# One ring of 1 MB weight pieces, adaLN split into steps by contraction tile and placed in the mixers, in a four-layer hybrid trunk on one core

## The reference, cut to what matters

```python
def trunk(x, cond, grid_rows, gla_s0, prm):
    for i in range(DEPTH):                       # 4 layers
        mod = (jax.nn.silu(cond) @ prm['w_ada'][i] + prm['b_ada'][i])[:, None, :]
        sh1, sc1, g1, sh2, sc2, g2 = jnp.split(mod, 6, axis=-1)
        h = rmsnorm(x, prm['norm_g'][i, 0]) * (1.0 + sc1) + sh1
        y = mixer_i(h)        # 0 Hyena convolution, 1 gated linear attention, 2 FNet, 3 pooling
        x = x + g1 * y
        h = rmsnorm(x, prm['norm_g'][i, 1]) * (1.0 + sc2) + sh2
        x = x + g2 * hier_moe(h, ...)            # 16 experts, two per token
    return rmsnorm(x, prm['final_g']), states
```

## Time and profile before

| what | value |
|---|---|
| median of 3 runs | 1601.7 us (1598.37 to 1603.82) |
| profiled execution | 1601.74 us, its span 1599.9 us |
| PE busy | 1414.2 us, 88% of the span |
| DVE, ACT, POOL busy | 394.0, 288.8, 100.7 us |
| DMA traffic | 552.35 MB of 10^6 bytes, mean 345 GB/s; 421 to 422 GB/s in the slices in which it never pauses |
| mean granted PE clock | 0.952 |

### The profile page before, as it was taken

How to read it: one execution, slowest core, us unless ns; L and a number is a source line. 1 busy time by engine, 2 the same in 40 slices (tenths; PEclk the granted TensorE clock), 3 DMA queues, 4 the chain that set the end, 5 groups by cost and what they waited for, 6 DMA issues and landing times.

```text
span 1599.9 us, 17267 instructions
## 1 busy us (share of the span) xinstructions
PE 1414.2 (88%) x7154; PEld 738.4 (46%) x7154; DVE 394.0 (25%) x904; ACT 288.8 (18%) x520; POOL 100.7 (6%) x105
## 2 busy tenths in 40 slices
PE   7999777799998799988799998888999865999986
PEld 3677335544432364857434433464444323444423
DVE  4333333412111320322411112123121124211112
ACT  2211000311010221112311101332110125111101
POOL 1000231110000100001100000011000012000001
PEclk9999978899999899999899999898999997899998
DMA  9877849489999976569499999685999996699995
GB/s 325 342 315 322 352 165 392 190 304 408 422 421 421 425 293 241 213 267 394 183 384 422 421 421 424 288 349 223 384 421 421 421 420 274 245 414 422 421 421 220
DMA packets 68671, 552.35 MB, mean 345 GB/s; under 512 B 7955, under 2 KB 8630, under 8 KB 10726
## 3 DMA queue, kind: packets, MB, share of 16 engines
q1 hardware_dynamic: 66266, 545.79, 83.0%
q0 software_dynamic: 1568, 4.55, 1.0%
q10 hardware_dynamic: 748, 0.74, 0.1%
HBM read 548.96 MB, written 2.10 MB: 344 GB/s over the span
## 4 chain that ended last, share of the span: by engine, by line
PE 71%; DMA 18%; DVE 6%; ACT 2%; issue 1%; POOL 1%; SPq 1%; DVEq 0%; POOLq 0%
PE bank L722 21%; DMA ring<-in_moe_w 15%; PE bank L671 12%; PE bank L746 10%; PE bank L631 6%; PE bank L690 4%; PE bank L706 3%; DMA ring<-in_w_ada 3%; PE bank L502 2%; PE bank L516 2%; PE bank L841 1%; PE bank L647 1%; PE bank L1008 1%; POOL hT L1827 1%; PE bank L904 1%
## 5 line engine op out<-in xcount | busy, mean ns | idle before, releaser
L722 PE MATMUL bank<-ring,arena 128*64 128x512 f32 x1024 | 236.9, 599 | 33.5 <-DMA ring<-in_moe_w 32.9
L722 PE MATMUL bank<-ring,hT 128*64 128x512 f32 x1024 | 226.3, 594 | 2.7 <-DMA ring<-in_moe_w 2.7
L746 PE MATMUL bank<-ring,arena 128*64 128x512 f32 x896 | 200.3, 596 | 0.2 <-DMA ring<-in_moe_w 0.2
L722 PEld LDWEIGHTS bank<-ring,arena 128*64 128x64 f32 x1024 | 68.6, 136 | 194.1 <-issue 125.2
L1419 DVE TENSOR_TENSOR rows<-rows,bank 128x512 f32<-128x512 f32 x32 | 22.0, 687 | 480.5 <-PE bank L722 480.5
L722 PEld LDWEIGHTS bank<-ring,hT 128*64 128x64 f32 x1024 | 71.7, 137 | 143.6 <-issue 134.5
L746 PEld LDWEIGHTS bank<-ring,arena 128*64 128x64 f32 x896 | 60.9, 137 | 119.6 <-issue 108.0
L671 PE MATMUL bank<-hT,ring 128*128 128x256 f32 x512 | 113.7, 383 | 1.7 <-DVE hT L1387 1.7
L631 PE MATMUL bank<-ring,condT 128*32 128x512 f32 x768 | 93.3, 641 | 16.8 <-DMA ring<-in_w_ada 16.8
L671 PEld LDWEIGHTS bank<-hT,ring 128*128 128x128 f32 x512 | 97.8, 192 | 15.8 <-issue 2.4
L1827 POOL TENSOR_TENSOR hT<-hT 128x256 f32<-128x256 f32 x48 | 34.7, 723 | 1029.2 <-ACT hT L1093 1026.0
(11 more groups left out here) (250 smaller groups left out, 1340.0 us busy)
## 6 DMA issues: line engine op xcount, KB each, us to landing
ring<-in_moe_w SPq DMA_DIRECT2D x368, 1024.0 KB, 18.1
ring<-in_w_ada SPq DMA_DIRECT2D x48, 2048.0 KB, 17.1
arena<-in_moe_w SPq DMA_DIRECT2D x16, 1024.0 KB, 23.4
ring<-in_hy_w_in SPq DMA_DIRECT2D x6, 2048.0 KB, 11.7
ring<-in_hy_w_out SPq DMA_DIRECT2D x2, 2048.0 KB, 19.1
ring<-in_gla_w_v SPq DMA_DIRECT2D x2, 2048.0 KB, 8.1
ring<-in_gla_w_g SPq DMA_DIRECT2D x2, 2048.0 KB, 8.1
ring<-in_gla_w_o SPq DMA_DIRECT2D x2, 2048.0 KB, 25.7
```

The source lines that it names most:

```text
L722: last = mm(bank[4 + kind][SLOTS * e:SLOTS * e + SLOTS, :], x[:, k, at:at + SLOTS], w[:, kk, e, :], start=k == 0, stop=k == KD - 1)
L746: last = mm(bank[6 + q // 2][SLOTS * e:SLOTS * e + SLOTS, :], hidT[:, f, SLOTS * e:SLOTS * e + SLOTS], w[:, ff, e, :], start=f == 0, stop= ...
```

## The change

The ring becomes 12 slots of 1 MB, used in strict turn by every piece. The mixers' weights are laid out in pieces of 256 columns in place of 512. An adaLN piece becomes one contraction tile k of all 2048 columns, so that eight pieces make a product, each used by itself in one step (4 matmuls) and freed by itself. The product (`ada(n, lo, hi)`) and the transposes (`ada_turned(n)`) stand apart on PE, as do `ada_rows` and `ada_mod` on DVE. Places: n = 0 before w_in; 1 to 4 in the Hyena convolution; 5 to 7 in GLA; 8 and 9 in FNet; 10 and 11 in pooling. n = 2 and 4 use bank 6, the others bank 7. The first gather of an expert stage uses banks 4, 6, 5, 6 in place of 4, 6, 7, 5, and its fourth part waits for the evacuation of its second. The arguments `beside` and, in `moe_round`, `turned` stand in the code and are not used.

The core of the diff:

```diff
-RING = 6
-PIECE = 4096
-SLAB = PIECE // 2
+RING = 12
+SLAB = 2048
...
+    before = [ada(0) + pieces("w_in", 12) + ada(1) + ada(2) + ada(3) + ada(4) + pieces("w_out", 4),
+              ada(5, 0, 5) + pieces("wq", 2) + ada(5, 5) + pieces("wk", 2) + pieces("wv", 4) + pieces("wg", 4)
+              + ada(6) + ada(7) + pieces("wo", 4),
+              ada(8) + ada(9) + pieces("fn", 4),
+              ada(10, 0, 5) + pieces("pool", 1) + ada(10, 5) + ada(11)]
...
+        experts = [("moe", i, p, kind, q) for p in range(PAIRS) for kind in range(3) for q in range(SLABS)
+                   if p or kind < 2]
+        for what in before[i] + [("first", i)] + experts + [("further", i)]:
...
-                return "ada_mm", 3 * what[1] + what[2] + 1
+                return "ada_mm", KD * what[1] + what[2] + 1
...
-                slots = [arrived(("ada", i, q, j)) for j in range(4)]
-                for k in range(KD):
+            def ada(n, lo, hi):
+                if lo == 0 and n:
+                    pe.wait_ge(s("mod_ready"), {2: 1, 3: 2, 4: 3}.get(n, n))
+                for k in range(lo, hi):
+                    w = arrived(("ada", n, k), 4)
                     for j in range(4):
-                        last = mm(bank[7][32 * j:32 * j + 32, :], condT[:, k, :], piece(slots[j], KD, 512)[:, k, :],
+                        last = mm(ada_bank(n)[32 * j:32 * j + 32, :], condT[:, k, :], w[:, j, :],
                                   start=k == 0, stop=k == KD - 1)
-                last.then_inc(s("ada_mm"), 1)
+                    last.then_inc(s("ada_mm"), 1)
+            def ada_turned(n):
                 pe.wait_ge(s("ada_rows"), n + 1)
...
             to_rows(0)
-            ada_at("w_in5")
+            ada(1, 0, 1)
             forward(0)
             to_rows(1)
-            ada_at("conv0")
+            ada(1, 1, 5)
             forward(1)
             inverse(0)
+            ada(1, 5, 8)
+            ada(2, 0, 3)
             to_rows(2)
+            ada_turned(1)
+            ada(2, 3, 4)
             forward(2)
             inverse(1)
+            ada(2, 4, 8)
+            ada(3, 0, 2)
             to_rows(3)
-            ada_at("conv1")
+            ada_turned(2)
+            ada(3, 2, 3)
             forward(3)
             inverse(2)
-            ada_at("conv2")
+            ada(3, 3, 8)
             inverse(3)
+            ada_turned(3)
+            ada(4, 0, 8)
             pe.wait_ge(s("z_ready"), 4)
-            residual(0, "w_out", rhs=uT)
+            residual(0, "w_out", rhs=uT, turned=4)
...
-        def first_gather(pre):
-            for t, b in enumerate((4, 6, 7, 5)):
+        def first_gather(pre, first):
+            for t, b in enumerate((4, 6, 5, 6)):
+                if t == 3:
+                    pe.wait_ge(s(pre + "xg_ready"), first + 2)
                 gather(pre, t, b)
...
+            ada(10, 0, 3)
             norm(6)
+            ada(10, 3, 5)
...
+            ada(11, 0, 8)
+            ada_turned(11)
             norm(7)
             moe(3)
```

More of the change, by code:

```diff
@@ L111, in constants @@
     return {k: v.astype(np.float32) for k, v in out.items()}
[L115 to L145, removed]
-            at += 1
[L148 to L158, removed]
-    return out
@@ L166, in build @@
+def build(nc, a):
+    stream = piece_stream()
+    where = {what: (slot, nth) for what, slot, nth in stream}
     ctx = ExitStack()
@@ L348, in source @@
                     "wk": "gla_w_k", "wv": "gla_w_v", "wg": "gla_w_g"}[k]
-            return a[name][what[1]]
+            return a[name][c]
         USED = ["h1_mm", "h3_mm", "y_mm"]
-        def landed(unit, part):
-            return s(f"{'fullb' if part else 'full'}{unit}")
         def expert_slab(n):
@@ L419, in _ @@
             last = {}
[L421 to L434, removed]
+            for what, slot, nth in stream:
                 if what[0] == "first":
@@ L469, in _ @@
                     continue
-                unit_free(unit, part)
-                src = source(what)
-                sp.dma_start(ring[unit][:, 0:src.shape[1]], src).then_inc(s(f"full{unit}"), 16)
-                last[unit, 0] = last[unit, 1] = freed(what)
+                if slot in last:
+                    name, value = last[slot]
+                    sp.wait_ge(s(name), value)
+                if what[0] == "moe":
+                    _, i, p, kind, q = what
+                    src = expert_slab(3 * SLABS * (PAIRS * i + p) + SLABS * kind + q)
+                else:
+                    src = source(what)
+                sp.dma_start(ring[slot][:], src).then_inc(s(f"full{slot}"), 16)
+                last[slot] = freed(what)
             for g, name in enumerate(("y_prompt", "y_sample")):
@@ L1325, in _ @@
[L1325 to L1334 removed]
+            norm(2)
+            shift(2)
@@ new lines, in _ @@
+            chain(last)
+            for b in range(2):
+                o_root = ors[:, 2 * b:2 * b + 2].rearrange("p h t -> p (h t)")
+                act_fn(o_root, o_root, ACT.Exp, scale=-0.5).then_inc(s("ors_ready"), 1)
+            residual(1, None, quarter)
+            moe(1)
+            norm(4)
+            shift(4)
+            for n in range(8):
+                act.wait_ge(s("mix_mm"), n + 1)
+                act_fn(fnp[:, n // 4, n % 4], bank[n % 4][:], ACT.Copy).then_inc(s("mix_rows"), 1)
@@ L1336, in _ @@
+            residual(3, "pool_b", half)
+            moe(3)
+            norm(2 * LAYERS)
             for g, name in enumerate(("y_prompt", "y_sample")):
```

800 lines of the change are left out of this document (403 added, 397 removed).

## The result

The changed kernel takes 1537.8 us in the median of 4 runs (1537.26 to 1539.11), against 1601.7 us (1598.37 to 1603.82): a ratio of 0.9604, with a 95% interval of 0.9586 to 0.9622. The forecast was 1538 us. The profiled execution took 1537.64 us, its span is 1535.8 us, 64.1 less than before.

The account below looks back on a forecast made before the run. No resource bounds throughout: PE and helpers pace mixers and routing, DMA the expert stages' second part. Terms -55.5 - 22.4 + 2.0 + 8 + 1.2 + 3 = -63.7 took 1601.7 to 1538 us; range 1524 to 1562.

Parts of the forecast that it names:

- Input projection: Hyena input projection: two adaLN blocks of 8.4 us each leave PE, -16.8 us.
- Convolution: Hyena convolution up to the residual: four adaLN products in steps instead of whole, 105.3 to 67.6 us, -37.7.
- The walk: Hyena convolution: operation-by-operation timing with assumed durations, DVE and POOL nearly back to back, giving 67.6 us.
- the rival that the steps don't fit: Hyena convolution: late pieces or delaying steps shrink the 37.7 us gain; kernel at 1557 or 1568 us; chance 0.15.
- The residual and the first expert stage: Hyena layer's end: residual -1.7 us on a busy PE, +0.7 for transposes; whole layer -55.5, gather +0.4.
- The rival that gains stay in the mixers: Expert stages: ring not full at their start, so DMA sets their end; about 1579 us; chance 0.05.
- GLA: GLA layer: three adaLN products instead of four, partly in waits, -22.4 us; +0.4 for the first gather's evacuation wait.
- FNet: FNet layer: n = 8 partly in waits, n = 9 ahead of the residual, +2.0 us; gather wait +0.4.
- Pooling: Pooling layer: two products added, 113 slabs without a DMA pause, +5.5 us, plus 2.5 for constants: +8.
- "+35 with nothing hidden": Whole kernel: no change, as pooling loses 35 us and the convolution gains none; 1602 us; chance 0.02.
- The rest: Expert stages: +1.2 us for gather evacuation waits, +3 for PE switching to and from steps' 32-column form.
- Load size: Ring loads, 2 MB to 1 MB: queued loads hide latency, against a 2.0 us fixed-cost rule estimating 132 us more.

## Why the prediction was right, step by step

- **Input projection, -16.8.** Measured: to_rows(0) 18.0 us earlier, of which 1.1 were there before the first adaLN product (a start that differs by chance): -16.9. The experiment that puts the two products back confirms 8.4 us a block.
- **Convolution, 105.3 to 67.6.** Measured 66.9. The walk with DVE and POOL back to back held; the rival that the steps don't fit is out. The experiment with whole products shows 20.8 of the 38.4 us to be the steps'. The walk took PE's durations from busy stretches (3.6 us for a forward), so it had the granted clock of 1.00 built in; the prediction named the clock only at the residual.
- **The residual and the first expert stage.** Predicted 55.1 up to the experts of layer 0 (-55.5, and 0.4 for the gather); measured 58.3, or 57.2 without the start: 2 us too little, of which the convolution has 0.7. All of it passed through: the last w3 slab of layer 0 is at 468.57 against 526.90. The rival that gains stay in the mixers is out in layers 0 to 2.
- **GLA, -22.0 with the gather.** Measured -18.1. This step was 4 us too good. I had said that five steps lie in the waits around the first norm. That wait was not idle time that a step can use: PE stands about 6 us at the branch over the fallback code, and only then begins the steps, at a granted clock of 0.53. From the last w3 slab to the gate products it takes 497.57 - 468.57 = 29.0 us, before 552.18 - 526.90 = 25.3.
- **FNet, +2.4 with the gather.** Measured +2.05, but out of two errors: the same loss ahead of the norm, and mixer products that ran faster. From the last w3 slab to FNet's first products it takes 3.6 us more (935.16 - 907.07 = 28.1, before 1007.64 - 983.15 = 24.5), and these products took 13.97 us in the chain, against 16.87 before. The clock granted over them is 1.00 in the changed kernel (935 to 949 us) and 0.81 before (1007 to 1024 us). Two steps stand right ahead of them now, and before, PE had been idle there but for the norm's few matmuls; no run takes these steps away and leaves the rest.
- **Pooling, +8.** Measured 284.75 - 275.16 = +9.6. DMA share 1.01 throughout, 421 GB/s: DMA is the bound as argued. The 283 us forecast were 1.6 too few; part of it is the rate of 113 slabs, 2.49 us each at 421 GB/s where I used 2.484. The bound is a narrow one: with one product less the layer still takes 280.5 us, 5.4 more than before. The rival "+35 with nothing hidden" is out.
- **The rest, +4.2.** From the first products to the last w3 slab, the expert stages of layers 0 to 2 are as long as before to 0.3 us. The step switches (+3) show nowhere as a term of their own, and layer 0 came out 2 us better than a sum that leaves them out.
- **Load size.** The row-based argument held: queued loads hide their completion. What I left out is that more and smaller loads can have a price all the same, about 0.07 us for each extra one at 0.5 MB. Whether going from 2 to 1 MB had one, no row shows: it doubled 66 of 435 loads of the ring, and the page's packets rise from 68671 to 78177.

The sum -63.7 against -63.9 in the medians is closer than the terms deserve, and that is luck: GLA's +4 and pooling's +1.6 were balanced by layer 0 (3.2 with the start) and by the +3 for step switches that never came.

## What to carry to other kernels

Split a stretch of work that is not urgent into steps as large as the waits it is to fill, so that it doesn't delay the chain that makes the waits (20.8 us here). That each step frees its own buffer belongs to it too, but no run has its share alone. Before a load is moved into an idle stretch of the ring, count the pieces that must land before the engine gets there, not only the pause: a pause behind the place of use is worth nothing to it (n = 10 in FNet, 13.7 us). And what a wait is put down to in the chain is only the last to come: behind the gap named after POOL stood a branch that ended almost with it, so the gap was no idle time for work placed ahead of the norm.

## What the runs showed of the hardware that I had not expected

- PE stands for 6.06, 5.82 and 5.97 us (the longest 6.1 in the waits above) after the expert stages of layers 0 to 2, at the branch over code that is not entered; without this code the gap is gone, and 9.6 us with it. An instruction queue moves a block in each gap (q8, one of 0.02 MB), which points to the fetch of instructions behind the jump; the wait for the value that decides it is not ruled out.
- 0.5 MB loads run at 409 GB/s with the DMA engines at a share of 1.03, 1 MB loads at 421 GB/s with 1.01. Packets or SP's issuing (27% of the chain): open.
- Three adaLN steps behind such a gap take 5.08, 4.41 and 4.27 us, where three take 2.71 behind busy stretches; over the first of these the granted clock is 0.53. Placed there, filler costs more than its size.
